# Stick-breaking scores over all 128 rows: the queries of even and odd heads in two tiles, each with zeros in the other half

## The reference, cut to what matters

```python
for start in range(0, S, BLOCK):
    z = einsum('bqhd,bkhd->bhqk', q[:, start:end], k[:, :end]) * SB_DIM ** -0.5
    before = s_idx < t_idx
    log_not = where(before, log_sigmoid(-z), 0.0)
    between = cumsum(log_not, axis=3, reverse=True) - log_not
    a = where(before, exp(log_sigmoid(z) + between), 0.0)
    outs.append(einsum('bhqk,bkhd->bqhd', a, v[:, :end]))
```

## Time and profile before

| what | us |
|---|---|
| median of 3 runs | 4196.78 |
| lowest and highest run | 4186.01, 4207.9 |
| span of the profiled execution | 4208.7 |
| TensorE busy, share of the span | 96% |
| VectorE busy, share | 61% |
| ScalarE busy, share | 37% |
| GpSimd busy, share | 13% |

### The profile page before, as it was taken

How to read it: one execution, slowest core, us unless ns; L and a number is a source line. 1 busy time by engine, 2 the same in 40 slices (tenths; PEclk the granted TensorE clock), 3 DMA queues, 4 the chain that set the end, 5 groups by cost and what they waited for, 6 DMA issues and landing times. The chain is left out here.

```text
span 4208.7 us, 50639 instructions
## 1 busy us (share of the span) xinstructions
PE 4024.5 (96%) x20617; PEld 3489.4 (83%) x20617; DVE 2562.5 (61%) x3863; ACT 1554.4 (37%) x2232; POOL 553.8 (13%) x397
## 2 busy tenths in 40 slices
PE   8999898899999899999999999999999999989998
PEld 7778797779999899999998887588888887678887
DVE  6432776679897875767766633675444442766443
ACT  3212125422666663323333234534232133644322
POOL 1000000000123332344322100101001110001000
PEclk9999999999999999999999999999999999999999
DMA  3344004334689799999983442133323434033332
GB/s 128 120 132 153 11 30 148 122 105 146 217 284 328 282 324 331 333 321 333 339 307 125 140 128 101 53 132 99 100 90 115 126 126 158 24 130 97 98 100 80
DMA packets 322163, 685.63 MB, mean 163 GB/s; under 512 B 19427, under 2 KB 77283, under 8 KB 319884
## 3 DMA queue, kind: packets, MB, share of 16 engines
q1 hardware_dynamic: 275852, 522.99, 37.0%
q0 software_dynamic: 36864, 134.23, 9.3%
q10 hardware_dynamic: 9216, 25.17, 1.5%
HBM read 581.37 MB, written 100.96 MB: 162 GB/s over the span
## 5 line engine op out<-in xcount | busy, mean ns | idle before, releaser
L1223 ACT CAST pe_w_high<-pe_w_raw 128x2048 fp32r<-128x2048 f32 (+1 forms) x168 | 316.3, 1883 | 523.8 <-DMA pe_w_raw<-in_peer_v 228.7
L1315 DVE TENSOR_TENSOR pe_w_low<-pe_w_raw,pe_w_high 128x2048 fp32r<-128x2048 f32 (+1 forms) x168 | 381.6, 2272 | 175.8 <-ACT pe_w_high L1223 175.4
L1111 PE MATMUL ps<-xn_p_high,pe_w_high 128*128 128x384 f32 (+1 forms) x1088 | 382.5, 352 | 34.1 <-DVE pe_w_low L1315 20.1
L2220 ACT CAST tail_w_high<-tail_w_raw 128x2048 fp32r<-128x2048 f32 (+3 forms) x124 | 221.4, 1790 | 445.1 <-DMA tail_w_raw<-in_w_in 145.7
L2229 DVE TENSOR_TENSOR tail_w_low<-tail_w_raw,tail_w_high 128x2048 fp32r<-128x2048 f32 (+3 forms) x124 | 266.5, 2153 | 186.2 <-ACT tail_w_high L2220 185.8
L1111 PE MATMUL ps<-xn_p_high,pe_w_low 128*128 128x384 f32 (+1 forms) x1088 | 373.0, 343 | 0.0
L1111 PE MATMUL ps<-xn_p_low,pe_w_high 128*128 128x384 f32 (+1 forms) x1088 | 372.9, 343 | 0.0
L1141 PE MATMUL ps<-pe_far_hidden_high,pe_w_high 128*128 128x384 f32 x1024 | 347.6, 339 | 26.3 <-DVE pe_near_hl L1441 23.9
L1141 PE MATMUL ps<-pe_near_hl,pe_w_high 128*128 128x384 f32 x1024 | 345.3, 337 | 0.0
L1141 PE MATMUL ps<-pe_far_hidden_high,pe_w_low 128*128 128x384 f32 x1024 | 345.2, 337 | 0.0
L1528 POOL DMA_INDIRECT home_pe_row<-in_peer_u,pe_expert x128 | 180.6, 1411 | 576.6 <-DVE pe_act L1501 379.4
(11 more groups left out here) (648 smaller groups left out, 9501.7 us busy)
## 6 DMA issues: line engine op xcount, KB each, us to landing
pe_w_raw<-in_peer_uT SPq DMA_DIRECT2D x64, 1024.0 KB, 7.9
pe_w_raw<-in_peer_v SPq DMA_DIRECT2D x64, 1024.0 KB, 7.6
in_w_raw<-in_w_in SPq DMA_DIRECT2D x34, 1024.0 KB, 5.7
tail_w_raw<-in_w_up SPq DMA_DIRECT2D x32, 1024.0 KB, 5.5
tail_w_raw<-in_w_down SPq DMA_DIRECT2D x32, 1024.0 KB, 5.2
pe_w_raw<-in_w_in SPq DMA_DIRECT2D x28, 1024.0 KB, 5.1
tail_w_raw<-in_w_in SPq DMA_DIRECT2D x28, 1024.0 KB, 5.1
dram_peer_hidden<-pe_rings_r ACTq DMA_DIRECT2D x64, 384.0 KB, 6.4
```

The source lines that it names most:

```text
L1111: last = pe.matmul(ps[:, q, 0:n], w[:, s, at], xp[:, 4 * i + c, 0:n], start=(i == 0 and c == 0 and p == 0), stop=(i == 1 and c == 3 and p ...
L1223: act.copy(ring.flat(hi, u), ring.flat(raw, u)).then_inc(w_hi, 1)
L1315: dve.tensor_tensor(ring.flat(lo, u), ring.flat(raw, u), ring.flat(hi, u).bitcast(F32), ALU.subtract).then_inc(w_lo, 1)
L2220: act.copy(hi, raw).then_inc(self.w_hi, 1)
```

## The change

The queries are loaded into two tiles. One holds the even heads on partitions 0 to 63 and zeros on 64 to 127, the other the odd heads on partitions 64 to 127 and zeros below. A score matmul then contracts all 128 rows: the keys of both heads of a slot against one head's queries beside zeros. The query load becomes two loads of 64 partitions. GpSimd zeroes the two other halves in the block of the latent attention, behind the tables and the wait for the stored projections, each memset behind a semaphore of the step before. The second query tile lies at 140.75 KB, 8 KB of a partition. The filler matmuls read the first tile.

```diff
         pool.tensor_copy(self.unit[:, :], self.k.ident[:, :])
-        pool.tensor_scalar(self.mask[:, :], self.causal[:, T - P:T], -1.0, NEG, ALU.mult, ALU.add)
+        pool.tensor_scalar(self.mask[:, :], self.causal[:, T - P:T], -1.0, NEG, ALU.mult, ALU.add).then_inc(self.prepared, 1)
...
             def _(pool):
                 suffix.prepare(pool)
+                ent.settled(pool)
+                for i, rows in enumerate(empty):
+                    pool.wait_ge(suffix.prepared, i + 1)
+                    pool.memset(rows, 0.0).then_inc(suffix.prepared, 1)
...
-                    r = slice(SBD * (h % 2), SBD * (h % 2) + SBD)
                     for kt in PARTS[i]:
                         b, c = bank[kt]
-                        pe.matmul(ps[:, b, c:c + wid[kt]], kT[r, h // 2, kt * P:(kt + 1) * P], qT[r, h // 2, kt * P:T],
+                        pe.matmul(ps[:, b, c:c + wid[kt]], kT[:, h // 2, kt * P:(kt + 1) * P], qT[h % 2][:, h // 2, kt * P:T],
                                   start=True, stop=False)
...
-                        pe.matmul(ps[:, 7, :], k.ident[:, :], qT[:, 0, :], start=True, stop=True)
+                        pe.matmul(ps[:, 7, :], k.ident[:, :], qT[0][:, 0, :], start=True, stop=True)
...
-                sb_q, sb_k, sb_v = (at(f"sb{l}_{n}", 161 + 8 * i, [P, 4, T]) for i, n in enumerate("qkv"))
+                sb_q = [at(f"sb{l}_q{half}", kb, [P, 4, T]) for half, kb in enumerate((161, 140.75))]
+                sb_k, sb_v = (at(f"sb{l}_{n}", 169 + 8 * i, [P, 4, T]) for i, n in enumerate("kv"))
+                own = [slice(SBD * half, SBD * half + SBD) for half in range(2)]
...
-                                 [(sb_q[:, :, :], p2[:, 0:4, :]), (sb_k[:, :, :], p2[:, 4:8, :]), (sb_v[:, :, :], tokens(pt2)[:, :, 0:GW])],
+                                 [*((sb_q[half][own[half], :, :], p2[own[half], 0:4, :]) for half in range(2)),
+                                  (sb_k[:, :, :], p2[:, 4:8, :]), (sb_v[:, :, :], tokens(pt2)[:, :, 0:GW])],
...
-                                 suffix)
+                                 suffix, [sb_q[half][own[1 - half], :, :] for half in range(2)])
```

More of the change, by code:

```diff
@@ L1643, in __init__ @@
     def __init__(self, k, name, at, kb, from_here, causal):
-        self.k, self.from_here, self.causal = k, from_here, causal
+        self.k, self.from_here, self.causal, self.prepared = k, from_here, causal, k.sem(name + "_prepared")
         self.suffix, self.total = at(name + "_suffix", kb, [P, P], F32R), at(name + "_total", kb + 0.5, [P, P], F32R)
@@ L1651, in prepare, with latent_attention @@
         pool.tensor_copy(self.unit[:, :], self.k.ident[:, :])
-        pool.tensor_scalar(self.mask[:, :], self.causal[:, T - P:T], -1.0, NEG, ALU.mult, ALU.add)
-def latent_attention(k, name, place, heads, outT, early, rotation, work, ent, suffix):
+        pool.tensor_scalar(self.mask[:, :], self.causal[:, T - P:T], -1.0, NEG, ALU.mult, ALU.add).then_inc(self.prepared, 1)
+def latent_attention(k, name, place, heads, outT, early, rotation, work, ent, suffix, empty):
     nc, ps = k.nc, k.ps
```

## The result

The changed kernel takes 4178.94 us, median of 22 runs (4166.29 to 4202.62), against 4196.46 for the kernel before (22 runs, 4182.32 to 4217.13). The ratio is 0.9953, 95% interval 0.9938 to 0.9967: 17.5 us between the medians, and 19.7 us by the ratio, between 14 and 26.

What follows compares the result with a forecast made beforehand. TensorE was taken to bound the stick-breaking loop, VectorE next. Per layer 2.57 + 0.70 + 3 x 0.96 = 6.15 us, 12.3 in both, taking the median from 4196.8 to 4184.5 us; range 4168 to 4200.

Steps and rivals of the forecast that it cites:

- The block: Each score block on TensorE, two score passes and a mask matmul: 0.24 us less, 0.96 a head.
- Heads 2 to 4: In the stick-breaking loop: each gives 0.96 us, the period on TensorE falling from 8.80 to 7.84.
- Head 1: In the loop: gives 0.70 us, 0.96 less a new 0.26 wait of head 4's scores for head 3's kept scores.
- Heads 5 to 7: End of the stick-breaking stage, without scores: waits stay at the same distance from the start of head 5.
- Head 0: Start of the loop: 0.79 us of slack before head 1's sums is gained; 0.17 of its 0.96 is lost.
- first stretch: TensorE scores heads 0 to 2: first sums 1.78 us earlier, head 1 2.57 with head 0's slack; clock unchanged.
- The 1.25 us of idle on VectorE: VectorE's wait per head for the first half of the sums: pays for 0.96, falling to about 0.3.
- rival 3: VectorE takes over earlier in the loop: heads 2 to 4 give only half, 9.4 us in all, 4187.4; chance 0.13.
- rival 1: The clock rises too in the first stretches, 1.7 and 3.3 us: 5 more, 4179.5; chance 0.12.
- Rival 2: Weight loads stay exposed with 128 rows, so a block costs what it did: 4196.8; chance 0.08.
- rival 4: Clock falls in the loop or retention, making the kernel slower; with fourteen more falls 11.5 us slower, 4208.3; chance 0.05.
- The two memsets: GpSimd zeroing in the latent attention's block: some 1.9 us each, 3.8 together, covered by 55 us.

Runs made afterwards that it cites:

- e5: Changed kernel plus one small bfloat16 matmul per score block, of 64 or of 128 rows: stage 80.2 and 80.3 us, or 74.9 and 75.0; one run each.
- e3_loop: Changed kernel with scores of heads 0 to 2 back at 64 rows, 128 rows only for heads 3 to 7: ratio to before 0.9992, stage 80.9 and 77.0 us.
- e7_cols: Changed kernel with the output matmuls also on the full array, 128 value columns instead of 64: ratio to before 0.9958, stage 73.4 and 73.5 us.
- e6_nofill: Changed kernel without the filler matmuls in the stage's first stretch: ratio to before 0.9960, stage 75.3 and 74.4 us.
- after_again: The changed kernel, unaltered, measured a second time: ratio to before 0.9957, stage 73.8 and 73.9 us.
- e8_pool_late: Kernel with full output columns, GpSimd's second remainder held back until head 6's arguments are written: ratio to before 0.9964, stage 72.7 and 72.8 us.

## Why the prediction was right, and what it missed

The direction and the mechanism of the blocks held; the size was 12.3 us forecast against 16.2 measured in the stage and 19.7 [14, 26] in the whole kernel, so the forecast gain lies below the interval. That the time fell into 4168 to 4200 says little, since that range holds no change too. What speaks for the prediction is the stage, term by term.

- The block: 0.14 from scores to mask at both widths, 0.10 before the scores, 0.11 behind a mask, as read off the latent attention. The 0.11 for the start behind the sums was in part luck: it was read off 64-column matmuls, and the scores here stand behind a 128-column float32r sum. The Trainium skill's rule that a load runs under a matmul in flight only where the row groups differ ("TensorE: Matmul & The Clock Gate", Part 3) does not hold here: 128-row loads ran 0.32 us ahead under 128-row matmuls, and the loads at a change of rows did not. With the Trainium skill's "TensorEngine Tiling (Array Packing)", Key Properties, that changing the tiling mode drains the engine, the runs agree as far as they show it: the way there and back measures 0.21 us in e5.
- Heads 2 to 4: forecast 0.96 less each, 0.98 measured. Head 1: 0.70 forecast, 0.77 measured. Its new wait in the scores is there, some 0.18 us (0.29 instead of 0.11 behind the sums) where I had 0.26. Heads 5 to 7 are unchanged (5.21 and 5.22).
- Head 0: the new wait stands at head 1's sums as foreseen, but its slack of 0.79 gave 0.65 where the first stretch was as before (e3_loop, layer 1). I let head 1's sums start as soon as the arguments are read; in the changed kernel they start 0.15 later.
- The 1.25 us of idle on VectorE shrank to nothing for heads 0 to 3, not to about 0.3, and 0.97 us of it was lost where GpSimd held VectorE up. That did not reach TensorE, so rival 3 did not come true: heads 2 to 4 gave all of their 0.98. There was luck in it: in head 6's softplus VectorE's third step began 0.04 us ahead of GpSimd's second remainder (2677.68 and 2677.72). In e7_cols the remainder came first, and VectorE and then TensorE waited.
- The term that was missing is the clock, and it was rival 1, given 0.12. I forecast the first stretch with the clock as it was. Up to head 1's first sums the gain was 3.7 and 5.2 us, where I had 2.57 for both. The two layers differ by 1.5 in this, which is the 1.5 by which 18.60 and 17.07 differed in the earlier trace rows. Against 6.15 forecast, the stage gave 7.4 and 8.9: 1.2 and 2.7 more, where rival 1 priced 1.7 and 3.3. The rest of that price did not come because ScalarE and VectorE now set the stretch's 13.84 us (e6_nofill). My argument against rival 1, that the loop has half-row scores too and shows 1.00, was wrong to lean on. The loop puts them between sums and outputs of all rows, which the first stretch has not; whether that is the reason was not tested.
- Rival 2 is refuted by the loads, rival 4 by the clock of 1.00 in both loops. In the retention the granted clock moves between profiles of one kernel (0.88 in layer 0 here, 0.84 in after_again over the same 42.28 us), so nothing there is put down to the change.
- Of the remaining difference of totals, 19.7 against 16.2, nothing is shown: it lies inside the interval.
- The two memsets took 3.67 us, forecast 3.8, and ended 54 us ahead of the stage; no wait for them or for the loads shows in the stage's timeline.

## What to carry to other kernels

Where TensorE is the bound, look for places that alternate between matmuls of 64 and of 128 rows: each way there and back cost 0.21 to 0.25 us here, and zeros in the unused rows cost no time (two passes of 512 columns read 1.12 us at 64 rows, 1.07 at 128). For columns, once a head, it was 0.27. Look for the same block elsewhere in the trace to price an unseen form; that gave the gain of a head to 2%. And ask of a change to TensorE what it does to the granted clock: by the difference from the forecast, it was about a quarter of the stage's gain (3.9 of 16.2 us). Before the next change, ask which engine comes next: e7_cols gave 0.46 of up to 1.9 us.

## What the runs showed that was not expected

- Half-row scores in the first stretch: a clock fall in 6 of 6 layers, with full-row scores and fillers in 0 of 14, two of them with the switches put back.
- GpSimd and VectorE held each other up on SBUF operands, and the one that began later paid. VectorE's float32 step of 1280 columns took 2.46 us instead of 1.49 when it began while GpSimd's remainder ran, and its cast 1.86 instead of 0.83 in e7_cols; GpSimd's own took 2.1 us in the kernel before and 2.59 in the changed one instead of 1.27, when VectorE had begun first. VectorE's arguments, which read PSUM too, kept their 1.09 beside a remainder. That e8_pool_late moved the remainder and got 1.49 back shows the cause.
- The code ahead of the changed stage's layer, the same in all kernels, took 2553 to 2572 us from profile to profile. A change of 0.4% can't be read from one span; it can from a stage.
